# Summing a modulation vector over partitions: one-column products against whole rows turned once

## The reference

```python
c_act = jax.nn.silu(c)
for l in range(DEPTH):                       # two layers of the second block
    shift, scale, gate = jnp.split(c_act @ w_ada[l] + b_ada[l], 3, axis=-1)
    h = rms_norm_2(x, norm_w[l]) * (1.0 + scale[:, None, :]) + shift[:, None, :]
    ...                                      # mixers on h, projected to y
    x = x + gate[:, None, :] * y
```

## Time and profile before

| | us |
|---|---|
| median of 3 runs | 2504.38 |
| lowest and highest | 2504.19, 2504.6 |
| profiled execution, its span | 2502.7 |
| TensorE busy | 2482.8 (99%) |
| VectorE busy | 1889.6 (76%) |
| ScalarE busy | 1236.4 (49%) |
| GpSimd busy | 22.9 (1%) |

### The profile page before, as it was taken

How to read it: one execution, slowest core, us unless ns; L and a number is a source line. 1 busy time by engine, 2 the same in 40 slices (tenths; PEclk the granted TensorE clock), 3 DMA queues, 4 the chain that set the end, 5 groups by cost and what they waited for, 6 DMA issues and landing times.

```text
span 2502.7 us, 33443 instructions
## 1 busy us (share of the span) xinstructions
PE 2482.8 (99%) x12605; PEld 2094.3 (84%) x12605; DVE 1889.6 (76%) x3358; ACT 1236.4 (49%) x1828; POOL 22.9 (1%) x39
## 2 busy tenths in 40 slices
PE   8999999999999999999999999999999999999999
PEld 7888888888888888878888869888888898888887
DVE  7888988898888888675555556666986767668865
ACT  4444444444444444445555456453455665544553
POOL 0000000000000000000000000000000000000000
PEclk9999999999999999999999999999999999999999
DMA  8787778777877786655545536444455544444554
GB/s 308 268 296 277 260 261 296 276 268 254 301 263 269 265 294 248 218 178 168 160 156 181 169 101 203 152 135 146 157 162 184 178 153 154 145 137 152 168 168 136
DMA packets 266545, 517.03 MB, mean 207 GB/s; under 512 B 16672, under 2 KB 21760, under 8 KB 265744
## 3 DMA queue, kind: packets, MB, share of 16 engines
q1 hardware_dynamic: 264144, 507.91, 59.6%
q0 software_dynamic: 1696, 6.47, 1.0%
q10 hardware_dynamic: 544, 0.52, 0.1%
HBM read 512.76 MB, written 2.10 MB: 206 GB/s over the span
## 4 chain that ended last, share of the span: by engine, by line
PE 88%; DVE 8%; issue 2%; ACT 2%; DMA 0%; DVEq 0%; SPq 0%; ACTq 0%
PE proj L590 14%; PE proj L592 14%; PE proj L591 14%; PE proj L1288 8%; PE proj L1290 8%; PE proj L1289 8%; PE scores L762 3%; DVE w_lo L1935 2%; DVE arena L2080 1%; PE proj L1280 1%; PE proj L1283 1%; PE proj L1282 1%; PE proj L630 1%; PE turn L769 1%; PE proj L621 1%
## 5 line engine op out<-in xcount | busy, mean ns | idle before, releaser
L1935 DVE TENSOR_TENSOR w_lo<-w_raw,w_hi 128x1024 fp32r<-128x1024 f32 (+1 forms) x739 | 896.4, 1221 | 278.8 <-ACT w_hi L1330 220.1
L1330 ACT ACTIVATE w_hi<-w_raw 128x1024 fp32r<-128x1024 f32 (+1 forms) x739 | 773.2, 1053 | 605.8 <-PE proj L592 368.8
L590 PE MATMUL proj<-w_hi,xt_lo 128*128 128x512 f32 x1628 | 648.8, 399 | 3.8 <-DVE w_lo L1935 3.7
L592 PE MATMUL proj<-w_hi,xt_hi 128*128 128x512 f32 x1628 | 635.3, 390 | 0.0
L591 PE MATMUL proj<-w_lo,xt_hi 128*128 128x512 f32 x1628 | 634.1, 389 | 0.0
L1288 PE MATMUL proj<-w_hi,xt_lo 128*128 128x512 f32 x976 | 395.6, 405 | 0.0
L1290 PE MATMUL proj<-w_hi,xt_hi 128*128 128x512 f32 x976 | 381.2, 391 | 0.0
L1289 PE MATMUL proj<-w_lo,xt_hi 128*128 128x512 f32 x976 | 380.5, 390 | 0.0
L590 PEld LDWEIGHTS proj<-w_hi,xt_lo 128*128 128x128 f32 x1628 | 306.0, 188 | 65.9 <-issue 4.2
L592 PEld LDWEIGHTS proj<-w_hi,xt_hi 128*128 128x128 f32 x1628 | 305.5, 188 | 65.5
L591 PEld LDWEIGHTS proj<-w_lo,xt_hi 128*128 128x128 f32 x1628 | 306.2, 188 | 59.9
(11 more groups left out here) (431 smaller groups left out, 2746.4 us busy)
## 6 DMA issues: line engine op xcount, KB each, us to landing
w_raw<-in_dsa_w_in_dram SPq DMA_DIRECT2D x159, 1024.0 KB, 7.4
w_raw<-in_w_in_dram SPq DMA_DIRECT2D x120, 1024.0 KB, 5.1
arena<-in_w_ada_dram SPq DMA_DIRECT2D x192, 512.0 KB, 6.0
w_raw<-in_w_out_dram SPq DMA_DIRECT2D x32, 1024.0 KB, 5.2
w_raw<-in_mla_w_in_dram SPq DMA_DIRECT2D x24, 1024.0 KB, 5.1
w_raw<-in_dsa_w_out_dram SPq DMA_DIRECT2D x16, 1024.0 KB, 5.0
w_raw<-in_mla_w_out_dram SPq DMA_DIRECT2D x16, 1024.0 KB, 5.0
w_raw<-in_mla_w_ukv_dram SPq DMA_DIRECT2D x8, 1024.0 KB, 5.5
```

What stands on the lines that cost most here:

```text
L590: mm(o, xt[1][:, k0 + kk, tok], WH[:, c % 2, k, 0:n], start=first, stop=False)
L592: ins = mm(o, xt[0][:, k0 + kk, tok], WH[:, c % 2, k, 0:n], start=False, stop=last)
L1330: A(hi[:, 2 * q:2 * q + 2, 0:n], RAW[:, c % 4, 2 * q:2 * q + 2, 0:n], ACT.Copy).then_inc(hi_made, 1)
L1935: V.tensor_tensor(lo[:, ks, 0:n], RAW[:, c % 4, ks, 0:n], hi[:, ks, 0:n].bitcast(F32), ALU.subtract).then_inc(lo_made, 1)
```

## The change

The sums over partitions are formed the other way around, and become columns later.

- A group's sum is one plain fp32 product: the stationary is 32 columns of ones, the moving operand the whole accumulator of 512 columns (`join_rows`). The result, 32 equal rows, goes to TP[1]. A join waits for VectorE's sum, for the last copy out of the bank, and for ScalarE's copy of the row before.
- Its slot (`ADA_END`) is three after that of the group's last piece, moved on where queries or keys are being turned; the last one comes at slot 323.
- ScalarE copies one row of TP[1] into `AROW` (one partition, 512 columns), one slot later (`ada_copies`).
- GpSimd's queue stores each row to a tensor in DRAM, and loads all 24 back as 96 rows of 128 (`AROWS`). TensorE turns them once, at slot 33 of the MLA stage (`turn_rows`), and VectorE's additions to `ADC` follow there, ahead of the first rotation of queries.
- `AROW` and `AROWS` lie in columns of `CST` that are used only from the second block on. These columns are no longer loaded at the start but from GpSimd's queue, after the rows have been turned. The constants' order changes for that, and TensorE and VectorE wait for the load ahead of the second block.
- The turns of queries, keys and y wait until earlier joins' rows have been copied out of TP[1]. Some semaphores are merged.

```diff
+ADA_GROUPS = DEPTH * ADA_COLS
+def ada_ends():
+    turns = {group_base(i, g) + d for i in range(DSA_ITERS) for g in range(GROUPS)
+             for at in (Q_TURN, K_TURN) for d in (at - 1, at)}
+    ends = []
+    for e in range(ADA_GROUPS - 1):
+        slot = ADA_AT[ADA_K * e + ADA_K - 1] + 3
+        while slot in turns:
+            slot += 1
+        ends.append(slot)
+    return ends + [group_base(DSA_ITERS - 1, 2) + 11]
+ADA_END = ada_ends()
+AT_ADA_ROWS = 33
...
+        ada_sums = nc.dram_tensor("ada_sums", [ADA_GROUPS, BW], F32, kind="Internal").ap()
+        AROW = CST[0:1, K_TRI + 2 * BW + 32:K_TRI + 3 * BW + 32]
+        AROWS = CST[:, K_TRI + 3 * BW + 32:K_TRI + 3 * BW + 160]
...
-            sp.dma_start(CST[:, K_MASK:K_END], io["constants"][:, K_MASK:K_END]).then_inc(cst_loaded, 16)
+            sp.dma_start(CST[:, K_MASK:K_TRI], io["constants"][:, K_MASK:K_TRI]).then_inc(cst_loaded, 16)
...
-            def columns(e, seen):
-                l, b = e // ADA_COLS, e % ADA_COLS
+            def join_rows(e):
                 pe.wait_ge(ada_summed, e + 1)
-                pe.wait_ge(max_found, seen + 1)
-                for q in range(4):
-                    at = 384 + 48 * l + 4 * b + q
-                    ins = mm(SP[:, at:at + 1], ACC[:, e % 2, q * P:(q + 1) * P], ONES[:, 0:1], start=True, stop=True,
-                             skip_group_check=True)
-                ins.then_inc(ada_columned, 1)
+                pe.wait_ge(ada_copied, e)
+                mm(TP[1][0:32, :], ONES[:, 0:32], ACC[:, e % 2, :], start=True, stop=True).then_inc(ada_joined, 1)
+            def turn_rows():
+                pe.wait_ge(turn_lo, 2 + 28)
+                pe.wait_ge(ada_moved, 16 * ADA_GROUPS + 16)
+                nc.tensor.transpose(TP[1][:, 0:P], AROWS, IDENT).then_inc(ada_joined, 1)
...
                             yield B + at
+                            pe.wait_ge(ada_copied, sum(p < B + at for p in ADA_END))
...
-                            summed(B + at, 4 * a)
...
-                            if k >= 4:
-                                summed(B + TICKS + 2 * k, 4 * a + 4)
-                summed(8 * DSA_HALVES, 48)
+            def ada_sums():
+                for e, slot in enumerate(ADA_END):
+                    yield slot
+                    q_before = sum(B + Q_TURN < slot for B in BASES)
+                    k_before = sum(B + K_TURN < slot for B in BASES)
+                    if q_before > k_before:
+                        pe.wait_ge(qt_copied, q_before)
+                    elif k_before > 0:
+                        pe.wait_ge(kt_copied, k_before)
+                    if e == ADA_GROUPS - 1:
+                        pe.wait_ge(turn_lo, 2 + 8 + 6)
+                    join_rows(e)
...
+                yield AT_ADA_ROWS
+                turn_rows()
...
+            def ada_copies():
+                for e, slot in enumerate(ADA_END):
+                    yield slot + 1
+                    act.wait_ge(ada_joined, e + 1)
+                    act.wait_ge(ada_moved, 16 * e)
+                    A(AROW, TP[1][0:1, :], ACT.Copy).then_inc(ada_copied, 1)
...
-                        dve.wait_ge(ada_columned, e - 1)
+                        dve.wait_ge(ada_joined, e - 1)
...
-                if slot == DSA_HALVES + 16:
-                    dve.wait_ge(ada_columned, DEPTH * ADA_COLS)
-                    dve.wait_ge(S("ada_rows"), 1)
-                    own(V.tensor_tensor(ADC[:, 0:96], ADC[:, 0:96], SP[:, 384:480], ALU.add))
...
                     yield up_start(i) + 2
+                    if i == 0:
+                        dve.wait_ge(ada_joined, ADA_GROUPS + 1)
+                        dve.wait_ge(tables_made, 3)
+                        own(V.tensor_tensor(ADC[:, 0:96], ADC[:, 0:96], TP[1][:, 0:96], ALU.add))
...
                     rope_q(0)
...
-            pool.wait_ge(ada_columned, DEPTH * ADA_COLS)
-            spread(LNG, io["ln_g"][0], par_loaded)
-            spread(LNB, io["ln_b"][0], par_loaded)
+            for e in range(ADA_GROUPS):
+                if e == ADA_GROUPS - 1:
+                    pool.wait_ge(ada_joined, ADA_GROUPS)
+                    spread(LNG, io["ln_g"][0], par_loaded)
+                    spread(LNB, io["ln_b"][0], par_loaded)
+                pool.wait_ge(ada_copied, e + 1)
+                pool.dma_start(ada_sums[e:e + 1, :], AROW).then_inc(ada_moved, 16)
+            pool.wait_ge(ada_moved, 16 * ADA_GROUPS)
+            pool.dma_start(AROWS[0:96, :], ada_sums.rearrange("e (q n) -> (e q) n", q=4)).then_inc(ada_moved, 16)
...
+            pool.wait_ge(ada_joined, ADA_GROUPS + 1)
+            pool.dma_start(CST[:, K_TRI:K_END], io["constants"][:, K_TRI:K_END]).then_inc(S("sums_loaded"), 16)
```

More of the change, by code:

```diff
@@ L80 @@
 X_AT = (1, 3, 5)
+BASES = [group_base(i, g) for i in range(DSA_ITERS) for g in range(GROUPS)]
 BUSY_SLOTS = {group_base(i, g) + d for i in range(DSA_ITERS) for g in range(GROUPS)
@@ L146 @@
 CLEAR_AT = 134
-K_ID, K_INV, K_MASK, K_TRI, K_TAIL, K_CH2, K_LEV, K_CHI, K_COL, K_LOW, K_UP, K_END = np.cumsum(
-    [0, 128, 64 + 32 + 64 + 2, 4 * 384, 128, 128, 256, 6 * 128, 4, 256, 128, 128]).tolist()
+K_ID, K_INV, K_MASK, K_CHI, K_TRI, K_TAIL, K_CH2, K_LEV, K_COL, K_LOW, K_UP, K_END = np.cumsum(
+    [0, 128, 64 + 32 + 64 + 2, 4 * 384, 4, 128, 128, 256, 6 * 128, 256, 128, 128]).tolist()
 K_SUM = K_END
@@ L319, in program @@
         mq_copied = sem("mq_copied")
-        rank_src, kp_src, kp_turned, kp_copied = sem("rank_src"), sem("kp_src"), sem("kp_turned"), sem("kp_copied")
+        kp_src, kp_turned, kp_copied = sem("kp_src"), sem("kp_turned"), sem("kp_copied")
         ada_loaded = [sem(f"ada_loaded{r}") for r in range(3)]
-        ada_used, ada_summed, ada_columned = sem("ada_used"), sem("ada_summed"), sem("ada_columned")
-        rows_loaded, rows_turned, c_ready = sem("rows_loaded"), sem("rows_turned"), sem("c_ready")
+        ada_used, ada_summed, ada_joined = sem("ada_used"), sem("ada_summed"), sem("ada_joined")
+        ada_copied, ada_moved = sem("ada_copied"), sem("ada_moved")
+        rows_loaded, rows_turned = sem("rows_loaded"), sem("rows_turned")
         affined, gate_spread, gate_copied = sem("affined"), sem("gate_spread"), sem("gate_copied")
@@ L830, in windows @@
                                 if a == 0:
-                                    pe.wait_ge(S("ada_rows"), 1)
+                                    pe.wait_ge(tables_made, 3)
                             else:
@@ L864, in y_turns @@
                         if g < 3 or t == 1:
+                            pe.wait_ge(ada_copied, ADA_GROUPS - (g < 3))
                             pe.wait_ge(turn_lo, 2 + 8 + min(2 * g + t, 6))
@@ L870, in y_turns @@
                         ins.then_inc(turned, 1)
-            side, turns = Side(windows()), Side(y_turns())
+            side, turns, sums = Side(windows()), Side(y_turns()), Side(ada_sums())
             for h in range(DSA_HALVES):
@@ L886, in _ @@
                     nc.tensor.transpose(TP[0][:, 0:P], PROWS, IDENT).then_inc(rows_turned, 1)
+                sums.upto(h)
                 side.upto(h)
@@ L903, in _ @@
                     half_chunk(C_DSA_OUT + n, B_DSA_OUT + b, j, q)
+                    sums.upto(DSA_HALVES + 2 * n + q)
                     side.upto(DSA_HALVES + 2 * n + q)
@@ L1253, in turn_h @@
                 ins.then_inc(turned, 1)
+            pe.wait_ge(S("sums_loaded"), 32)
             for l in range(LAYERS):
@@ L1445, in dsa_evac @@
                 act.sem_inc(act_evacuated, 1)
-            side, turns = Side(windows()), Side(y_turns())
+            side, turns, copies = Side(windows()), Side(y_turns()), Side(ada_copies())
             for h in range(DSA_HALVES + 32):
@@ L1471, in _ @@
                         act.sem_inc(act_evacuated, 1)
+                copies.upto(slot)
                 side.upto(slot)
@@ L1928, in _ @@
             V.memset(ONES[:, :], 1.0).then_inc(warm, 1)
+            own(V.memset(AROWS[96:128, :], 0.0))
             def low_half(c, q, n=BW):
@@ L2046, in tables_of @@
             def tables_of():
-                dve.wait_ge(sin_made, 1)
+                dve.wait_ge(tables_made, 1)
                 sq = TMP[:, 0:320]
@@ L2062, in tables_of @@
                 own.sync()
-                dve.wait_ge(c_ready, 1)
+                dve.wait_ge(tables_made, 2)
             def ada(slot):
@@ L2324, in heads @@
                         yield AT_KP[0]
-                        dve.wait_ge(rank_src, 1)
+                        dve.wait_ge(kp_turned, 1)
                         for t in range(T):
@@ L2351, in heads @@
                     yield up_start(i) + 2
+                    if i == 0:
+                        dve.wait_ge(ada_joined, ADA_GROUPS + 1)
+                        dve.wait_ge(tables_made, 3)
+                        own(V.tensor_tensor(ADC[:, 0:96], ADC[:, 0:96], TP[1][:, 0:96], ALU.add))
+                        own.sync()
+                        dve.sem_inc(ada_summed, 1)
```

(6 more changed lines are left out.)

20 lines of the change are left out of this document (7 added, 13 removed).

## The result

The change made the kernel slower: 2510.37 us (median of 9 runs, 2510.29 to 2511.72) against 2504.54 us (9 runs beside them), a ratio of 1.0023, 95% interval 1.0014 to 1.0032. That is 5.8 us more, where 2.4 us less were forecast; it is outside the range.

A forecast was written before the change was run, and what follows sets the result against it. TensorE's stream was taken to bound the kernel. Removed 21.6 + 1.64 + 0.21 = 23.45 us, added 20.9 + 0.13 = 21.0, so -2.4 from 2504.38 to 2502.0 us; range 2499.1 to 2505.5, forecast's chance 0.68.

The forecast's parts named there:

- So an edge is about 0.01 us, and a join 0.87 us: First mixer, joins: priced from plain fp32 scores set between projections; 24 joins add 20.9 us.
- The upper bound of 0.94: First mixer: dearest price of a join, with the 0.08 us extra step seen behind a turn; 24 joins 22.6 us.
- Exposed edges (slower): Rival at the joins: neither weight load runs ahead, 0.42 us a join, 10.1 us, 2512.1 us; chance 0.08.
- The stream of a join: First mixer: one plain fp32 product of 512 moving columns takes 0.86 us, as at L621.
- The old groups: First mixer: each removed group of column sums cost 0.90 us of TensorE's stream, 24 of them 21.6 us.
- The stalls of the earlier trace: First mixer: two TensorE waits for VectorE at the column sums, 0.62 and 1.02 us, vanish; 1.64 us gained.
- the third rival: First mixer: VectorE's lag stays and shows at weights instead of sums; +1.64 us, 2503.6 us; chance 0.10.
- May take back some tenths: Around 800 us: without the stalls VectorE is again close behind TensorE and may cost some tenths.
- The turn of the rows: MLA stage: one transposition more on TensorE, 0.11 us, say +0.13 with an edge.
- The copies and the row stores: ScalarE's 24 copies, about 0.59 us each, cost zero; GpSimd's DMA issues, 0.67 us each, on a nearly idle engine.
- the rival on GpSimd: Each DMA issue holds VectorE for 0.67 us, felt at three places; +2.0 us, 2504.0 us; chance 0.06.
- The start: First 40 us: taken as zero; rival says transfers bound it, 2.6 us come free, 2499.4 us; chance 0.08.

The follow-up runs named there:

- e1_wide: Changed kernel with the join's stationary 128 columns of ones instead of 32; 2503.68 us (10 runs), ratio 0.9995 to the kernel before.
- e8_light: e1_wide with three pieces of VectorE's sums (12 instructions, slots 244 to 246) left out; 2503.46 us (one run).

## Why the prediction was wrong, step by step

*Which step failed.* "So an edge is about 0.01 us, and a join 0.87 us", carried over from the scores. The scores are the same type in the same place, but their stationary has 128 columns, and the join's had 32. No row of before has a narrow stationary in plain fp32, and the prediction called the scores "the same kind of product" without a word on the width. The edges of a join are 0.31 us together, not 0.01: 24 x 0.31 = 7.5 us. The upper bound of 0.94 was taken from what follows a turn, again 128 columns wide, so it bounded nothing. The rule of the Trainium skill on tiling modes (TensorEngine Tiling (Array Packing), "Tiling Modes"), which speaks against this very product, was not weighed.

*The rival that named it.* "Exposed edges (slower)" had the mechanism (neither the join's load nor the next projection's runs ahead) and about the size: 0.42 a join and 2512.1 us, where 0.31 and 2510.37 were measured. But the cause that it named was wrong (waits on three semaphores and two switches of type): e1_wide keeps all of those and has no edges. Because the scores, which share these causes, spoke against it, it got 0.08.

*The stream of a join*, 0.86 us from the earlier trace rows: right. The two records stand 0.43 us apart in every kernel here, and with a wide stationary the whole join is 0.883.

*The old groups*: 0.90 forecast, 0.905 measured.

*The stalls of the earlier trace rows*: 1.64 us were counted as gone for good. In the kernel after they came back in part as late weights, as the third rival said. (A third wait of 0.15 us, at the group of 396.86, was overlooked; it went too.) Its timeline:

```profile
801.38 0.39 PE L615 MATMUL proj<-w_hi,xt_hi 128*128 128x512 f32 x1
802.19 0.50 PE L613 MATMUL proj<-w_hi,xt_lo 128*128 128x512 f32 x1 [0.43 <-DVE w_lo L1978]
```

A step of 0.81 us instead of 0.23, and two longer ones at 798.34 and 798.73: 0.96 us together with the restarts behind them. In e1_wide, whose stream is quicker, it is 1.4. "May take back some tenths" was too little; TensorE waits for the same VectorE, only one instruction further on. That it is VectorE was tried on e1_wide, by e8_light.

*The sum with the measured terms*, step by step over the same matmuls, half chunk 8 to 343: the joins add 28.0 us (forecast 20.9), the old groups with their waits take 23.5 away (forecast 23.2), late steps elsewhere add 0.9: +5.45. The 28.0 are taken join by join: the first fills an older wait and costs 0.85, the others 1.11 to 1.20. For e1_wide the same sum is 20.6 - 23.5 + 1.4 = -1.5. The turn of the rows lies behind this stretch and adds 0.09 (forecast 0.13).

*What held.* No join waits for ScalarE or VectorE, the turn of rows does not wait, and the first MLA turn is not late. The copies and the row stores are as cheap as forecast, by groups of the kernel after (times, busy us, mean ns, idle before):

```profile
L1458 ACT ACTIVATE constants<-turn 1x512 f32<-1x512 f32 x24 | 13.9, 578 | 0.5 <-ACT arena L1431 0.5
L3110 POOL DMA_DIRECT2D ada_sums<-constants x24 | 11.9, 494 | 960.3 <-ACT constants L1458 960.3
```

An issue took 0.49 us instead of 0.67. Of VectorE's weight halves, the 16 that overlap one of these issues last 1.224 us in the mean and the other 304 that start before 1015 us 1.224 too: an issue doesn't hold VectorE, and the rival on GpSimd falls for this change. The start didn't gain: the DMA share of the first 40 us fell from 0.97 to 0.91, and half chunk 8 came no sooner in any kernel, so that rival falls too.

*The range.* It ended at 2505.5 with the only rival outside it at 0.08. An operation that no row shows, made 24 times on the engine that bounds the kernel, should have had the price of both loads within the range.

## What to carry to other kernels

Price a matmul from a row that has its type, its moving size and the width of its stationary; where one of the three has no row, put two loads that don't run ahead, and the gap that each leaves, into the range. Widening a stationary of equal columns to 128 cost nothing here and gained 7 us, and in fp32r a narrow one cost its stream alone. Look at the waits of the weight loads as well as at those of the matmuls. When an engine that is 88% busy causes a stall, taking away the instruction that waited can move the stall to the next one, as here; less work on that engine removed it (e8_light).

## What the runs showed of the hardware

- A plain fp32 product with 32 or 64 stationary columns is exposed at both sides, 0.27 us (ahead of a turn) to 0.33 us together, behind and ahead of every other kind of product tried, and not between two of its own kind (0.875 us for the second). In the list of waits its edges show only at the weight loads, as idle time of "issue" (24 times at L826), and not at the matmuls. Why the chip does so, no run here shows.
- The same 32 columns in fp32r cost 0.229 us for 512 moving columns, between projections and ahead of a wide plain fp32 product.
- A subtraction of GpSimd over 512 columns (1.08 us at best, 2.07 at worst) and VectorE's weight halves and sums hold each other, up to 0.89 us on a weight half of 1.22; DMA issues on GpSimd's queue held nothing.
